# The second block's mixer: k's norm moved into the shift stage, the attention's input tiles behind it, block-diagonal operands built by ScalarE too, one root for all attention norms

## The reference, cut to what matters

```python
h = rms_norm(x, mix_norm)
p = h @ w_in                                    # 14 + 12 + 16 column blocks of 128
p_rwkv = token_shift(p[..., :SHIFT_COLS], mu)   # r, k, v, w_lo, a_lo, g_lo
# RWKV-7 half
decay = exp(-exp(-softplus(-(w0 + tanh(w_lo) @ w_up)) - 0.5))
a = sigmoid(a0 + a_lo @ a_up);  g = sigmoid(g_lo) @ g_up
kk = k * k_k;  kk = kk / max(sqrt(sum_per_head(kk * kk)), 1e-12)
k = k * (1 + (a - 1) * k_a)
y = rwkv7_recurrence(r, decay, k, v, -kk, kk * a)   # state S = S diag(w) + (S a) b^T + v k^T
y = (normalised(y) * lnx_g + lnx_b + sum_per_head(r * k * r_k) * v) * g
# attention half (fox): q, k, v, f_lo from 12 column blocks and 8 columns
q = rms_norm(q, q_norm);  k = rms_norm(k, k_norm)   # per head of 64
o = softmax(q k^T / 8 + c_t - c_s, causal) v        # c = cumsum(log_sigmoid(f_lo + bias))
x = x + (gate_a * (y @ rwkv_proj) + gate_b * (o @ fox_proj)) @ w_out
```

## Time and profile before

| | us |
|---|---|
| median of 3 runs | 3009.7 (3008.61 to 3010.69) |
| the profiled execution's own time | 3010.91 |
| its span, first to last instruction | 3008.9 |
| TensorE busy | 2778.5 (92% of the span) |
| VectorE busy | 1878.3 (62%) |
| ScalarE busy | 1236.3 (41%) |
| GpSimd busy | 770.4 (26%) |
| mean granted TensorE clock | 0.949 of full |

### The profile page before, as it was taken

How to read it: one execution, slowest core, us unless ns; L and a number is a source line. 1 busy time by engine, 2 the same in 40 slices (tenths; PEclk the granted TensorE clock), 3 DMA queues, 4 the chain that set the end, 5 groups by cost and what they waited for, 6 DMA issues and landing times.

```text
span 3008.9 us, 43543 instructions
## 1 busy us (share of the span) xinstructions
PE 2778.5 (92%) x17592; PEld 2511.3 (83%) x17592; DVE 1878.3 (62%) x3207; ACT 1236.3 (41%) x1674; POOL 770.4 (26%) x333
## 2 busy tenths in 40 slices
PE   8989999999999988699999999999799868897898
PEld 7869999998888865599999988888797757785896
DVE  5655997776555556659977765555654674405554
ACT  3434463334545443344633344454443512132443
POOL 0001987663000000029966630000000230042000
PEclk9999999999999997699999999999899978898999
DMA  5554554445666642155544456665455410032454
GB/s 199 163 179 155 172 179 155 141 141 168 192 193 190 193 154 89 56 174 176 170 154 141 141 177 192 191 191 193 133 183 182 132 60 1 1 98 87 156 183 141
DMA packets 122919, 449.55 MB, mean 149 GB/s; under 512 B 13728, under 2 KB 13856, under 8 KB 122592
## 3 DMA queue, kind: packets, MB, share of 16 engines
q1 hardware_dynamic: 120800, 439.47, 45.7%
q0 software_dynamic: 1920, 7.30, 0.8%
HBM read 445.67 MB, written 1.05 MB: 148 GB/s over the span
## 4 chain that ended last, share of the span: by engine, by line
PE 88%; DVE 7%; POOL 3%; ACT 2%; issue 1%; DMA 0%; DVEq 0%; SPq 0%; POOLq 0%; ACTq 0%
PE ps L418 12%; PE ps L419 12%; PE ps L420 12%; PE ps L464 10%; PE ps L466 10%; PE ps L465 10%; PE ps L531 4%; DVE W L1198 4%; PE ps L616 3%; PE ps L440 2%; POOL lo L1803 2%; PE ps L441 2%; PE ps L442 2%; DVE x L1198 1%; PE ps L404 1%; DVE small L1198 1%
## 5 line engine op out<-in xcount | busy, mean ns | idle before, releaser
L853 ACT ACTIVATE hi<-ring 128x1024 fp32r<-128x1024 f32 x830 | 878.6, 1059 | 1277.0 <-PE ps L420 645.3
L1221 DVE TENSOR_TENSOR lo<-ring,hi 128x1024 fp32r<-128x1024 f32 x544 | 665.7, 1225 | 603.6 <-ACT hi L853 603.4
L418 PE MATMUL ps<-xT_r,hi 128*128 128x256 f32 x3248 | 935.4, 288 | 12.5 <-POOL lo L1803 9.4
L419 PE MATMUL ps<-xT_r,hi 128*128 128x256 f32 x3248 | 920.9, 284 | 0.0
L420 PE MATMUL ps<-xT_r,lo 128*128 128x256 f32 x3248 | 920.5, 283 | 0.0
L1803 POOL TENSOR_TENSOR lo<-ring,hi 128x1024 fp32r<-128x1024 f32 x286 | 725.4, 2543 | 588.5 <-ACT hi L853 588.5
L418 PEld LDWEIGHTS ps<-xT_r,hi 128*128 128x128 f32 x3248 | 624.1, 192 | 15.7 <-issue 6.4
L419 PEld LDWEIGHTS ps<-xT_r,hi 128*128 128x128 f32 x3248 | 624.6, 192 | 0.7 <-issue 0.7
L420 PEld LDWEIGHTS ps<-xT_r,lo 128*128 128x128 f32 x3248 | 623.8, 192 | 0.0
L464 PE MATMUL ps<-hi,oht_r 128*128 128x512 f32 x1040 | 411.5, 396 | 14.5 <-DVE W L1198 14.5
L466 PE MATMUL ps<-hi,oht_r 128*128 128x512 f32 x1040 | 408.8, 393 | 0.0
(11 more groups left out here) (213 smaller groups left out, 2883.3 us busy)
## 6 DMA issues: line engine op xcount, KB each, us to landing
ring<-in_peer_u SPq DMA_DIRECT2D x256, 512.0 KB, 3.5
ring<-in_peer_v SPq DMA_DIRECT2D x256, 512.0 KB, 4.2
ring<-in_f SPq DMA_DIRECT2D x132, 512.0 KB, 3.5
ring<-in_ret_vg SPq DMA_DIRECT2D x32, 512.0 KB, 3.5
ring<-in_peer_q SPq DMA_DIRECT2D x32, 512.0 KB, 3.5
ring<-in_ret_qk SPq DMA_DIRECT2D x16, 512.0 KB, 4.2
ring<-in_ret_out SPq DMA_DIRECT2D x16, 512.0 KB, 4.0
ring<-in_in_shift SPq DMA_DIRECT2D x14, 512.0 KB, 4.2
```

The source lines that it names most:

```text
L418: pe.matmul(o, h, xT[:, k, 0:256], start=k == 0, stop=False)
L419: pe.matmul(o, h, xT[:, k, 256:512], start=False, stop=False)
L853: hid.done(a.activation(hi[m % NH][:, :], ring[j % NR][:, :], ACT.Copy), j)
L1221: lo_v.done(v.tensor_tensor(lo[m % NH][:, :], ring[j % NR][:, :], as32(hi[m % NH][:, :]), ALU.subtract), j)
```

## The change

It rewrites the first part of the mixer, on all engines, as straight code in place of woven generators.

- k's squares and their sums (`kk_sq`, `kk2`) are made after the fourth and fifth pair of shift tiles, the square root after the sixth, the reciprocal (128x1024) after the sixth on VectorE, and the product with kk after the seventh.
- All 12 `in_fox` tiles stand before the masked products: four before the LoRA products, eight between them and `bonus`. Six of them are split by VectorE in place of two.
- The block-diagonal operands a, r and v are multiplied in place by VectorE (a, r) and scattered by ScalarE, two instructions each, and b and k stay VectorE's.
- The four roots of the attention's norms are one: the squares of q and k go to 32 columns, and one `power` of 128x32 follows. The gains of the norms are applied as a scalar per partition when the transposed q and k are copied.
- The attention begins four rounds after the first masked product, and thus goes beside the masked products; before, it began beside the last of them.

```diff
-        add("in_fox", i, "V" if i < 2 else "P")
+        add("in_fox", i, "V" if i < 6 else "P")
...
+        M_wf, M_mkp = selT[:, 0:64], selT[:, 64:64 + MK]
+        M_fz = [oht[0:8, 1536:1792], oht[0:8, 1792:2048], fzt[0:8, :]]
+        M_rr = sm[:, 64:96]
...
+                for i in range(7):
+                    mat_t([TILE["in_shift", 2 * i + j] for j in range(2)], "mix", "shift", i, among=RW, first=i == 0)
+                    if i == 4:
+                        pe.wait_ge(*at(dve, "kk_sq"))
+                        head_sums("kk2", M_kn)
+                fox_in(0)
+                pe.wait_ge(*at(act, "lora_in"))
+                pe.wait_ge(*loaded("lora"))
...
+                fox_in(1)
+                fox_in(2)
+                pe.wait_ge(*at(dve, "rk"))
+                head_sums("bonus", M_tmp)
+                b = bank("fox_f", among=FX)
+                pe.wait_ge(*loaded("fox"))
...
                 def rwkv():
-                    for i in range(7):
-                        mat_t([TILE["in_shift", 2 * i + j] for j in range(2)], "mix", "shift", i, among=RW, first=i == 0)
-                        yield
-                    res.add("shift")
-                    yield
...
-                    yield
-                    yield
-                    for c in range(0, 4, 2):
-                        b = bank("kk2", c, among=RW)
-                        pe.wait_ge(*at(dve, "kk_sq"))
-                        for j in range(2):
-                            ins = pe.matmul(b[:, j * 256:j * 256 + 256], C("bdones"), c4(M_tmp)[:, c + j, :], start=True, stop=True)
-                        mm.done(ins, "kk2", c)
-                    yield
...
                     pe.wait_ge(*at(dve, "bd"))
+                    pe.wait_ge(*at(act, "bd"))
...
-                    while "shift" not in res:
-                        yield
-                    for z in range(3):
-                        yield from mat_n([TILE["in_fox", z * 4 + j] for j in range(4)], "mix", "fox_p", z, among=FX)
-                        yield
-                        if z < 2:
-                            yield
...
+                    for z, name in enumerate(("fox_q", "fox_k")):
+                        pe.wait_ge(*at(dve, "fox_qk", z, 1))
+                        parts(name, lambda tt, c: tok3(M_fnat[z], tt, c), 4, among=FX)
+                        yield
                     yield
-                    pe.wait_ge(*at(dve, "fox_qk", 1, 1))
-                    parts("fox_q", lambda tt, c: tok3(M_fnat[0], tt, c), 4, among=FX)
                     yield
-                    parts("fox_k", lambda tt, c: tok3(M_fnat[1], tt, c), 4, among=FX)
-                    yield
-                    while "o" not in res:
-                        yield
...
+                    if i == 5:
+                        a.wait_ge(*at(dve, "kk_norm", 2))
+                        act.done(a.activation(M_kn, M_kn, ACT.Sqrt), "kk_norm")
+                a.wait_ge(*at(dve, "shift", 6))
+                act.done(a.activation(M_P[0:32, 12, :], M_P[0:32, 12, :], ACT.Tanh))
+                act.done(a.activation(M_P[0:96, 13, :], M_P[0:96, 13, :], ACT.Sigmoid), "lora_in")
+                a.wait_ge(*at(pool, "zero_bd"))
+                block_diagonal(4, M_P[:, 8:12, :].rearrange("p c t -> p (c t)"), "bd_v")
+                fox_in(0, range(4))
+                for c in range(0, 4, 2):
+                    for name, dst, bias in (("w_up", M_lgd, "w0"), ("a_up", M_av, "a0")):
+                        a.wait_ge(*at(mm, name, c))
...
+                fox_in(1, range(2))
+                a.wait_ge(*at(dve, "decay"))
+                act.done(a.activation(M_eP, M_eP, ACT.Exp), "decay_p")
+                act.done(a.activation(M_eL, M_Lc, ACT.Exp), "decay_l")
+                act.done(a.activation(M_eN, M_Lc, ACT.Exp, scale=-1.0), "decay_n")
+                fox_in(1, range(2, 4))
+                a.wait_ge(*at(dve, "bd_a"))
+                block_diagonal(0, M_eP, scale=-1.0)
+                a.wait_ge(*at(dve, "bd_r"))
+                block_diagonal(1, M_P[:, 0:4, :].rearrange("p c t -> p (c t)"), "bd")
+                fox_in(2, range(4))
...
+                def squares(z):
...
+                    for tt in range(2):
+                        nv = M_fnat[z][:, tt, :].rearrange("p (h d) -> p h d", h=8)
+                        sqf = oht[:, 0:512].rearrange("p (h d) -> p h d", h=8)
+                        v.wait_ge(*at(act, "fox_p", z, tt))
+                        tt_(sqf, nv, nv, ALU.mult)
+                        red_(M_rr[:, (z * 2 + tt) * 8:(z * 2 + tt) * 8 + 8], sqf, ALU.add)
...
+                    if i == 3:
+                        for c in range(4):
+                            ts_(c4(M_kk)[:, c, :], k_[:, c, :], pc("kk", c), None, ALU.mult)
+                        tt_(M_kn, M_kk, M_kk, ALU.mult, name=("kk_sq",))
+                    if i == 4:
+                        for c in range(0, 4, 2):
+                            v.wait_ge(*at(mm, "kk2", c))
+                            ts_(c4(M_kn)[:, c:c + 2, :], j2(ps("kk2", c)), 1e-24, None, ALU.max, name=("kk_norm", c))
+                            empties(dve, "kk2", c)
+                    if i == 5:
+                        v.wait_ge(*at(act, "kk_norm"))
+                        step(v.reciprocal, M_kn, M_kn)
+                    if i == 6:
+                        tt_(M_kn, M_kn, M_kk, ALU.mult)
+                for j in range(4):
+                    split(TILE["in_fox", j] + 2)
...
+                    stt_(c4(M_tmp)[:, c, :], r_[:, c, :], pc("rk", c), c4(M_kk)[:, c, :], ALU.mult, ALU.mult, name=("rk",))
+                tt_(M_av, M_av, M_kn, ALU.mult)
+                v.wait_ge(*at(act, "decay_p"))
+                tt_(M_eP, M_eP, M_kn, ALU.mult, name=("bd_a",))
+                v.wait_ge(*at(act, "decay_l"))
+                tt_(flat(r_), flat(r_), M_eL, ALU.mult, name=("bd_r",))
+                v.wait_ge(*at(act, "decay_n"))
+                v.wait_ge(*at(pool, "zero_bd"))
+                for h in range(2):
+                    bd = [M_BD[i][h * 64:h * 64 + 64, :, h * 64:h * 64 + 64] for i in (2, 3)]
+                    tt_(bd[0], u16(M_av, h), u16(M_eN, h), ALU.mult)
+                    tt_(bd[1], u16(M_kk, h), u16(M_eN, h), ALU.mult, name=("bd",))
+                step(v.tensor_copy, M_pC, M_eL.rearrange("p (u t) -> p u t", u=16)[:, :, 63])
+                squares(0)
+                squares(1)
+                ts_(M_rr, M_rr, 1.0 / 64, RMS_EPS, ALU.mult, ALU.add, name=("var", "fox"))
+                for c in range(0, 4, 2):
+                    v.wait_ge(*at(mm, "bonus", c))
+                    tt_(c4(M_bon)[:, c:c + 2, :], j2(ps("bonus", c)), v_[:, c:c + 2, :], ALU.mult)
+                    empties(dve, "bonus", c)
+                v.wait_ge(*loaded("masks"))
...
-                    v.wait_ge(*at(act, "kk_norm"))
-                    step(v.reciprocal, M_kn, M_kn)
...
-                    v.wait_ge(*at(act, "decays"))
-                    v.wait_ge(*at(pool, "zero_bd"))
-                    for h in range(2):
-                        bd = [M_BD[i][h * 64:h * 64 + 64, :, h * 64:h * 64 + 64] for i in range(5)]
-                        stt_(bd[0], u16(M_kn, h), -1.0, u16(M_eP, h), ALU.mult, ALU.mult)
-                        tt_(bd[1], u16(flat(r_), h), u16(M_eL, h), ALU.mult)
-                        tt_(bd[2], u16(M_av, h), u16(M_eN, h), ALU.mult)
-                        tt_(bd[3], u16(M_kk, h), u16(M_eN, h), ALU.mult)
-                        step(v.tensor_copy, bd[4], u16(flat(v_), h), name=("bd",))
-                    step(v.tensor_copy, M_pC, M_eL.rearrange("p (u t) -> p u t", u=16)[:, :, 63], name=("chunk_decay",))
-                    res.add("o")
...
-                            yield
-                        if z < 2:
-                            for tt in range(2):
-                                nv = M_fnat[z][:, tt, :].rearrange("p (h d) -> p h d", h=8)
-                                v.wait_ge(*at(act, "fox_p", z, tt))
-                                tt_(sqf, nv, nv, ALU.mult)
-                                red_(rr, sqf, ALU.add)
-                                rsqrt(rr, rr, 1.0 / 64, RMS_EPS, "fox", z, tt)
-                                tt_(nv, nv, b3(rr, [128, 8, 64], 2), ALU.mult)
-                                yield
-                                v.wait_ge(*loaded("fox"))
-                                tt_(nv, nv, b3(M_nrm[:, z * 64:z * 64 + 64], [128, 8, 64], 1), ALU.mult, name=("fox_qk", z, tt))
+                    def scaled(z):
+                        for tt in range(2):
+                            nv = M_fnat[z][:, tt, :].rearrange("p (h d) -> p h d", h=8)
+                            rr = M_rr[:, (z * 2 + tt) * 8:(z * 2 + tt) * 8 + 8]
+                            tt_(nv, nv, b3(rr, [128, 8, 64], 2), ALU.mult, name=("fox_qk", z, tt))
+                    def turned(name, dst, gain):
+                        v.wait_ge(*at(mm, name, "T", 0))
```

(10 more changed lines are left out.)

247 lines of the change are left out of this document (85 added, 162 removed).

## The result

The changed kernel takes 3022.3 us (median of 6 runs, 3020.66 to 3024.96), the kernel before beside it 3010.2 us (6 runs): a ratio of 1.004, 95% interval 1.003 to 1.005. It is 12 us slower, where I had forecast 12 us faster, and outside the range. The profiled execution took 3021.14 us, its span 3019.0 us.

What follows compares the result with a forecast made beforehand. TensorE was taken as the bound, busy 92% of the span. Stage terms 9.4 - 2.9 + (105 - 114.7 - 16.6) + 8.2 = -11.6 us at `fx_out` took 3010.9 to 2999, median 2998; range 2973 to 3015.

Steps and rivals of the forecast that it cites:

- The stall of 5.3 us: Behind the shift stage: TensorE waits for VectorE's `lo`, queued behind the reciprocal, from 2379.5 until 2384.8 us.
- The second wait: Two attention tiles later: TensorE waits 3.8 us for the third tile's `hi` and `lo`, behind ScalarE's tanh, sigmoid and scatters.
- Bounds: 0 and 6 x 2.2 = 13 us; I take 3: Operands, before the first masked product: surcharge for six GpSimd `lo` and VectorE instructions blocking each other, taken as 3 us.
- The other surcharge: Operands, before the first masked product: attention tiles running at the lower clock after waits, 3 us in all.
- I take 68 (bounds 61 and 83): Masked products with attention beside them: 61 us at full clock, taken as 68 because the clock falls in part.
- The rest is bare ... 18 us: Levels left without attention pairs: 8.1 us per half, 5.5 in the last level, summed as 18 us at full clock.
- the factor of 1.14: Levels: measured over full-clock time before, put down to the clock of 0.80; it turned 92 us into 105.
- Its last two chunks find no gate tile ...: +4.5, less 1.1 that was seen before: Gate stage: the recurrence's last two chunks cannot hide copies and VectorE's state update behind gate tiles; +4.5 less 1.1 us.
- +4.9 us of TensorE: Gate stage: `Vs` and three groups of `bdT`, done before in the stage of 16.6 us, fall into it.
- rival 2: Masked products with attention run at 1.2 GHz: 83 us in place of 68, total 3013, no change; chance 0.16.
- rival 1: Clock stays near full from the first masked product on: 61, 92, 86 for 68, 105, 89; total 2975; chance 0.17.
- Rival 3: Attention tiles run cold: all 12 at 4.95 us, total 3020; decides from 8 tiles on; chance 0.12.

Runs made afterwards that it cites:

- the version without it: Changed kernel with the last six `lo` of the attention tiles made by VectorE in place of GpSimd: 3020.6 us, ratio 1.0034 to the kernel before.
- all but the placement: Kernel before with all parts of the change, attention tiles and scores left woven where they were: 2997.2 us, ratio 0.9956.
- the three edits of the front: On the changed kernel: all `lo` by VectorE (3020.6 us), last two tiles' `hi` ahead of ScalarE's scatters (3021.8), reciprocal behind first six `lo` (3021.9); together 3015.7.
- the other: Kernel before with all parts woven and bonus last (2991.1 us), plus `Vs` and the eight transposes moved into the half levels: 3000.7 us, ratio 0.9972.
- The same kernel: Changed kernel with `Vs` and transposes in the half levels, three front edits, and useless products ahead of four waits beside the masked products: 2987.5 us, ratio 0.9929.
- the version with the turned operands alone: Changed kernel with `Vs` and the eight groups of operand transposes put into the ten half levels: 2999.4 us, ratio 0.9970.

## Why the prediction was wrong

The sum was -11.6 us at `fx_out`; measured +10.5. By its own steps:

- **Shift stage and attention tiles: right, in part by luck.** The stall of 5.3 us is 5.06 (2384.41), LoRA starts at 2399.30 for 2400.2. The second wait was 1.58 us for 3.8, mostly because the tiles ahead of it ran cold (7.65 us for two, where 5.8 were forecast): the two cancel.
- **"Bounds: 0 and 6 x 2.2 = 13 us; I take 3": mis-sized.** The lock with GpSimd took 8 us of VectorE's chain, as the version without it shows (k chain 11.6 to 5.4 us, decay 2.0). I had put the hits behind the instruction that ScalarE waits for; they fell ahead of it, and ScalarE's queue carried them on: scatters at 2425.36 for 2418, `hi` behind them, the eleventh tile at 2434.02 for 2425.8. (The 0.69 us taken from the earlier trace rows is of an instruction with a PSUM input; one with two SBUF inputs takes the same at 2437.66 us of the changed kernel.) The other surcharge, 3 us for cold tiles, was 4.5 (7.65 and 8.46 us for two tiles each). With the forget gate at 7.07 us for 5.1, the first masked product was at 2451.2, not 2445: +6.2 us.
- **"I take 68 (bounds 61 and 83)": 73.0.** The mechanism was named, the clock was lower than taken (0.66). At 0.84 the stage takes 63.7 us with fillers in it, near my 61 for the full clock. +5.0 us.
- **Levels, "The rest is bare ... 18 us": added wrongly.** One and a half halves of 8.1 and two of 5.5 are 23.2 us. At the factor of 1.14 that is 6 of the 7 us that were missing (112.0 for 105). The halves themselves fit: the two full bare ones took 9.97 and 8.56 us, one of the last level 6.3, for 9.2 and 6.3 forecast.
- **Gate stage: the wait right, the work mis-sized.** "Its last two chunks find no gate tile ...: +4.5, less 1.1 that was seen before" is 3.4 us; TensorE's idle time behind the last gate tile rose from 1.1 to 4.6 us. What was too low is "+4.9 us of TensorE": it is busy 7.4 us longer in the stage, at a clock of 0.91 for 0.96. The two tails, changed and before:

```profile
2705.49:2729.10 23.61, 19.04 (x121) 18.30 (x120) 2.82 (x7) 3.98 (x9) 1.03 (x1) 0.73 0.07 23
2713.13:2718.62 5.49, 4.38 (x40) 4.18 (x40) 1.38 (x2) 2.45 (x5) 0.00 (x0) 1.00 0.31 98
```

The tail is 18.1 us longer and its products run at 0.73, while the tiles ahead of it are over 6.0 us sooner, 69.3 us for 75.4. The stage is 92.9 us for 89. The step also took these 8 us as given, where they hang on the order: ten pieces moved into the levels take 13.3 us off the stage.

Those four errors are 6.2, 5.0, 7.0 and 3.9 us, 22.1 together, and all have one sign. None passes its own bounds; I took the bounds of the whole from one rival at a time. The nearest was rival 2: with 0.66 in the masked products, some two thirds of the stage ran at 1.2 GHz, for a third of that rival's price (5 of 15 us). For rival 1 I had read "0.91 and more in stages with tiles", but the earlier trace rows have 0.88 and 0.71 in two of the four stages with tiles. Rival 3 was seen in four tiles (7.65 and 8.46 us for two each), not in eight.

What the change is worth by its parts, as measured: all but the placement -13 us; the rest of it, the placement above all, +25, of which holding the scores back takes away 14, and moving Vs and the transposes takes away 23 by the medians (these overlap). Why the three edits of the front gave 5.8, 5.2 and 2.5 us at the first masked product and 1.7, 0.5 and 0.4 us in the median (less than the spread of their runs) is only argued: in all three profiles the levels are 3.0 us and the gate stage 2.4 us longer than in the changed kernel's, at clocks of 0.79 and 0.88 for 0.81 and 0.91, with the same instructions. What sets the clock to one value or the other there stays open.

## What to carry to other kernels

When an engine's work is moved earlier, ask what stood beside it before and what will stand beside it now: half the attention came to stand beside masked products that were over in 38 us without it, and small pieces that had been hidden beside its end came to stand ahead of a serial chain. Short independent pieces belong into the waits of a chain, well ahead of what needs them, but only while that chain is what ends last: the same move gained 23 us by the medians in one version and lost 10 in the other. Before a gain is read from one profile, compare it with a profile that has the same instructions in the same stretch: here these differed by up to 4.4 us. And where a sum has four terms with a common cause, widen the range for all moving together.

## What the hardware showed beside this

- Useless products in TensorE's waits shortened a stage from 72.96 to 63.65 us, the granted clock going from 0.66 to 0.84. In the changed kernel TensorE stood still 2.27, 4.38 and 3.65 us ahead of three of its transposes there, and a pair of them took 0.66 us; with products ahead, 0.38 and 0.44 us. The Trainium skill (TensorE: Matmul & The Clock Gate, "HAM oscillation — how this bites in real kernels") describes waits between bursts that throttle the array each time. The rows agree for the second and third of these waits, with an engine's chain in the place of a transfer; ahead of the first the granted clock had already fallen, at 2470.5 us, 1.6 us before the wait began.
- The same kernel came in two groups of times: 2977.8 to 2981.2 us and 2993.8 to 2995.9, the first at a mean granted clock of 0.961, the second at 0.954; the version with the turned operands alone did the same (0.955 to 0.956, and 0.948 to 0.952). In which stage they differ was not seen, since only one execution of each kernel has a profile.
- A VectorE instruction with one full SBUF operand and a per-partition scalar (128x256, from W and `col`) took 2.38 us beside GpSimd's `lo` for 0.35 alone, 2.0 us longer, as one with two operands was (2.52 for 0.43). The Trainium skill (SBUF — State Buffer, "Who interferes with whom") counts `tensor_scalar` among those that can take the shared ports, on conditions on its operands; the rows agree.
- GpSimd's power on 128x32 took 5.44 us, on 128x8 1.66: four times the width, 3.3 times the time.
